# Query and key heads of one attention layer, normalized and rotated with tokens on the partitions

## What is computed

```python
def rms_norm(x, g):
    y = xf * lax.rsqrt(jnp.mean(xf * xf, axis=-1, keepdims=True) + EPS)
    return (y * g.astype(jnp.float32)).astype(x.dtype)

def apply_axial_rope(x, cos, sin):
    xs = x.reshape(x.shape[:3] + (2, 2, HEAD_DIM // 4))
    x1, x2 = xs[..., 0, :], xs[..., 1, :]
    out = jnp.stack([x1 * c - x2 * s, x2 * c + x1 * s], axis=-2)

bg_l, cg_l, vc_l, q_l, k_l, v_l, gt_l = jnp.split(hx @ w_in[layer], SPLITS, axis=-1)
q_l, k_l, v_l = split_heads(q_l, k_l, v_l, q_norm_g[layer], k_norm_g[layer])
q_c, k_c, v_c = split_heads(q_c, k_c, v_c, q_norm_g[layer], k_norm_g[layer])
q_l = apply_axial_rope(q_l, cos, sin)
k_l = apply_axial_rope(k_l, cos, sin)
k_all = jnp.concatenate([k_c, k_l], axis=1)
o_l = latent_attention(q_l, k_all, v_all)
```

## Time and profile before

| | us |
|---|---|
| median of 3 runs | 1324.51 |
| lowest, highest | 1324.28, 1335.15 |
| the profiled execution's own time | 1324.45 |
| its span, first to last instruction | 1322.6 |
| PE busy | 1304.7 (99%) |
| DVE busy | 903.0 (68%) |
| ACT busy | 644.3 (49%) |
| POOL busy | 27.3 (2%) |

### The profile page before, as it was taken

One profiled execution on the slowest core, in us unless ns is written; L12 is line 12 of the kernel. 1 busy time (PEld: TensorE's weight loads), 2 busy tenths in 40 slices (PEclk: granted clock), 3 DMA queues, 4 the chain that ended last, 5 costly groups with the idle time before them and its releaser, 6 DMA issues. The chain is left out here.

```text
span 1322.6 us, 23508 instructions
## 1 busy us (share of the span) xinstructions
PE 1304.7 (99%) x9348; PEld 1210.0 (91%) x9348; DVE 903.0 (68%) x1455; ACT 644.3 (49%) x1027; POOL 27.3 (2%) x27
## 2 busy tenths in 40 slices
PE   9999999999999999999999999999999999999998
PEld 6788888888889999999999999989999999999998
DVE  4768775555658587554775555788887665689873
ACT  4622311222236345554555445666665765556552
POOL 0000000000010000000000000200000000100000
PEclk9999999999999999999999999999999999999999
DMA  9755555646635354545556665556546455436760
GB/s 358 270 186 191 191 191 192 222 159 215 204 107 161 111 159 130 159 128 160 178 155 194 190 201 174 171 159 184 148 143 181 128 174 176 145 112 208 217 197 33
DMA packets 201485, 230.20 MB, mean 174 GB/s; under 512 B 7073, under 2 KB 191649, under 8 KB 201377
## 3 DMA queue, kind: packets, MB, share of 16 engines
q1 hardware_dynamic: 201088, 228.42, 54.7%
q10 hardware_dynamic: 288, 0.28, 0.1%
HBM read 227.63 MB, written 1.05 MB: 173 GB/s over the span
## 5 line engine op out<-in xcount | busy, mean ns | idle before, releaser
L1105 PE MATMUL P<-XHB,WH 128*128 128x256 f32 (+1 forms) x1808 | 553.1, 306 | 7.4 <-DVE XLB L1784 3.9
L1106 PE MATMUL P<-XLB,WH 128*128 128x256 f32 (+1 forms) x1808 | 543.2, 300 | 0.0
L1107 PE MATMUL P<-XHB,WL 128*128 128x256 f32 (+1 forms) x1808 | 543.2, 300 | 0.0
L1988 DVE TENSOR_TENSOR WL<-W,WH 128x1024 fp32r<-128x1024 f32 x358 | 431.7, 1224 | 87.2 <-ACT WH L1565 87.0
L1565 ACT ACTIVATE WH<-W 128x1024 fp32r<-128x1024 f32 x358 | 369.0, 1042 | 249.3 <-PE P L1107 157.8
L1105 PEld LDWEIGHTS P<-XHB,WH 128*128 128x128 f32 x1808 | 340.0, 188 | 27.7 <-issue 8.2
L1106 PEld LDWEIGHTS P<-XLB,WH 128*128 128x128 f32 x1808 | 340.1, 188 | 15.2 <-issue 0.5
L1107 PEld LDWEIGHTS P<-XHB,WL 128*128 128x128 f32 x1808 | 340.2, 188 | 14.6
L1105 PE MATMUL P<-GH,WH 128*128 128x256 f32 (+1 forms) x372 | 121.2, 326 | 0.0
L1106 PE MATMUL P<-GL,WH 128*128 128x256 f32 (+1 forms) x372 | 120.6, 324 | 0.0
L1107 PE MATMUL P<-GH,WL 128*128 128x256 f32 (+1 forms) x372 | 120.6, 324 | 0.0
(11 more groups left out here) (322 smaller groups left out, 1797.3 us busy)
## 6 DMA issues: line engine op xcount, KB each, us to landing
W<-in_ffn_w_in SPq DMA_DIRECT2D x88, 512.0 KB, 4.8
W<-in_w_in_ab SPq DMA_DIRECT2D x72, 512.0 KB, 4.6
W<-in_w_modt SPq DMA_DIRECT2D x56, 512.0 KB, 3.9
W<-in_w_in SPq DMA_DIRECT2D x52, 512.0 KB, 4.1
W<-in_ffn_w_out SPq DMA_DIRECT2D x40, 512.0 KB, 4.8
W<-in_w_in_c SPq DMA_DIRECT2D x32, 512.0 KB, 4.3
W<-in_w_out_ab SPq DMA_DIRECT2D x16, 512.0 KB, 4.4
W<-in_w_out_c SPq DMA_DIRECT2D x16, 512.0 KB, 4.7
```

Of the source, the lines that this page charges most:

```text
L1105: pe.matmul(o, h[:, k, c], xh[:, kk, a:b], start=kk == 0, stop=False)
L1106: pe.matmul(o, h[:, k, c], xl[:, kk, a:b], start=False, stop=False)
L1107: mm = pe.matmul(o, l[:, k, c], xh[:, kk, a:b], start=False, stop=kk == gm.nk - 1)
L1988: dve.tensor_tensor(l, a, h.bitcast(F32), ALU.subtract).then_inc(S["wl"], 1)
```

## The change

q and k are now made with the tokens on the partitions (`turned=False`: the activation is the stationary operand, the weights stream), as v was already. The columns of the weights are permuted on the host so that the swap of the rotation is a reversal of two halves of 64 along the row. The norm of a head is now a sum along the row. `qk_norm(u)` handles one gemm at a time (u = 0 to 3: two query heads, two token blocks; u = 4: both key heads, four token blocks) and is appended after q 0, q 1, q 2, q 3 and v:

- `qs`: ACT squares 128x128 pieces with an accumulated row sum (4 for a unit of q, 8 for k), then one root over 4 or 8 columns.
- `qr`: DVE takes a small reciprocal, then for each rotated piece a product with the sine table (halves reversed, into MC) and a product with the cosine table (in place); four of each. For k also four products with the gain alone. All are scalar_tensor_tensor with the reciprocal as the per-partition scalar.
- POOL adds the two parts of the rotation, two adds of 128x256 for a unit, ten in all.
- `qt`: PE transposes the pieces back (4 of 128x128 for a unit of q, 4 for each key head, 24 in all) and waits before it for the unit's last add on POOL. ACT copies the result to Q or K, 128x512 each.

The tables (gain times sine and cosine) are made once by DVE in a step `qg`, during the last products of the feed-forward, from a new transfer of 128 x 512 numbers on SP's queue. The k gemm writes four tiles of 256 columns instead of two of 512. The one-hot tile and POOL's two memsets are gone.

The core of the diff:

```diff
-            if i % 2:
-                self.call(lambda i=i: self.back.append(self.qk_norm(i // 2)))
+            self.call(lambda i=i: self.back.append(self.qk_norm(i)))
         self.call(self.reach, "ctx")
-        self.gemm("k", 0, WIN, 0, 8, 4096, ALL, first=True)
+        self.gemm("k", 0, WIN, 0, 8, 4096, ALL, turned=False, first=True)
...
-    def qk_norm(self, s):
-        self.step("qs", a=s)
-        for _ in range(2):
+    def qk_norm(self, u):
+        self.step("qs", a=u)
+        yield
+        self.step("qr", a=u)
+        yield
+        yield
+        for v in range(2 if u == 4 else 1):
+            b, f = self.bank(self.up("qn"))
+            self.step("qt", a=u, b=v, bank=b, free=f)
+            for name in (("k", v),) if u == 4 else (("q", 2 * u), ("q", 2 * u + 1)):
+                self.ready.add(name)
+                self.end[name] = self.at("qn")
             yield
-        b, f = self.bank(self.up("qr"))
-        self.step("qa", a=s, bank=b, free=f)
-        for _ in range(3):
-            yield
-        todo = None
-        for i in range(4):
-            if todo is not None:
-                self.rope(*todo)
-                todo = None
-            b, f = self.bank(self.up("qn"))
-            self.step("qb", a=s, b=i, c=self.at("qn"), bank=b, free=f)
-            if s < 2 or i % 2:
-                todo = (s, i, self.at("qn"))
-            else:
-                self.ready.add(self.name(s, i))
-                self.end[self.name(s, i)] = self.at("qn")
-            yield
-            yield
-        if todo is not None:
-            self.rope(*todo)
-
...
+            sp.dma_start(GR, w["qkg"].partition_broadcast(128).rearrange("p o c -> p (o c)")).then_inc(SX[0], 16)
...
-                elif s.kind == "qa":
-                    pe.wait_ge(S["fill"], 2)
-                    for i in range(4):
-                        n = 4 * s.a + i
-                        pe.wait_ge(S["qs"], n + 1)
-                        pe.matmul(ps[:, 0:T], HOT[:, 3 - i:131 - i], SQ[:, n % 3, T * (n // 3 % 2):T * (n // 3 % 2) + T], start=i == 0,
-                                  stop=i == 3).then_inc(S["qh"], 1)
-                elif s.kind == "qb":
+                elif s.kind == "qt":
                     pe.wait_ge(SI[5], 16)
-                    if s.b == 0:
-                        pe.wait_ge(S["qi"], s.a + 1)
-                    pe.matmul(ps[:, 0:T], con("sel", 128 * s.b, 128 * s.b + 128),
-                              rows_of(s.a), start=True, stop=True).then_inc(S["qb"], 1)
-                elif s.kind == "rope":
-                    ap = head(s.a, s.b)[0]
-                    pe.wait_ge(S["qn"], s.c)
-                    pe.matmul(ps[:, 0:T], con("perm"), ap, start=True, stop=True).then_inc(S["rm"], 1)
+                    n = 4 if s.a == 4 else 2
+                    pe.wait_ge(S["rd"], 2 * s.a + 2)
+                    for h in (s.b,) if n == 4 else (0, 1):
+                        for j in range(n):
+                            c = 128 * j if n == 4 else 256 * h + 128 * j
+                            mm = pe.transpose(ps[:, c:c + 128], place(s.a, j)[:, 128 * h:128 * h + 128], con("id"))
+                    mm.then_inc(S["rm"], 1)
...
+                if name == "s2":
+                    for u in range(5):
+                        k = 4 if u == 4 else 2
+                        for j in (k - 2, k - 1):
+                            y, p = raws(u)[j][1], place(u, j)
+                            pool.wait_ge(S["ro"], 8 * u + 2 * k + 2 * (j % 2) + 2)
+                            pool.tensor_tensor(p, p, y, ALU.add).then_inc(S["rd"], 1)
...
@@ -1640,17 +1617,26 @@
                         square("s6", k, (X[:, k, 256:512], 1.0))
                 elif s.kind == "qs":
                     act.wait_ge(S["on"], stat["s2"][2] + 6)
-                    for i in range(4):
-                        ap, _, _, (name, v) = head(s.a, i)
-                        n = 4 * s.a + i
-                        act.wait_ge(S[name], v)
-                        if n >= 6:
-                            act.wait_ge(S["qh"], n - 5)
-                        act.activation(SQ[:, n % 3, T * (n // 3 % 2):T * (n // 3 % 2) + T], ap, ACT.Square).then_inc(S["qs"], 1)
-                elif s.kind == "qa":
-                    act.wait_ge(S["qh"], 4 * s.a + 4)
-                    act.activation(rows_of(s.a), ps[:, 0:T], ACT.Sqrt, scale=1.0 / 128, bias=con("eps")) \
+                    n = 4 * s.a
+                    for j, y in raws(s.a):
+                        act.wait_ge(S["ke" if s.a == 4 else "qe"], j + 1 if s.a == 4 else 2 * s.a + j + 1)
+                        for h in range(2):
+                            if n >= 12:
+                                act.wait_ge(S["qs"], n - 11)
+                            act.activation(SQ[:, n // 4 % 3, 128 * (n % 4):128 * (n % 4) + 128], y[:, 128 * h:128 * h + 128],
+                                           ACT.Square, accum_out=RQ[:, n:n + 1]).then_inc(S["qs"], 1)
+                            n += 1
+                    act.wait_ge(S["qs"], n)
+                    act.activation(RQ[:, 4 * s.a:n], RQ[:, 4 * s.a:n], ACT.Sqrt, scale=1.0 / 128, bias=con("eps")) \
                         .then_inc(S["qr"], 1)
+                elif s.kind == "qt":
+                    if s.a < 4:
+                        act.wait_ge(S["rm"], s.a + 1)
+                        act.activation(Q[:, 2 * s.a:2 * s.a + 2, :], ps.rearrange("p (h t) -> p h t", h=2), ACT.Copy) \
+                            .then_inc(S["qn"], 1)
+                    else:
+                        act.wait_ge(S["rm"], 6)
+                        act.activation(K[:, s.b, :], ps, ACT.Copy).then_inc(S["qn"], 1)
...
-                elif s.kind == "qa":
-                    r = rows_of(s.a)
-                    dve.wait_ge(S["qr"], s.a + 1)
-                    dve.reciprocal(r, r).then_inc(S["qi"], 1)
-                elif s.kind == "qb":
-                    ap, gain, _, _ = head(s.a, s.b)
-                    dve.wait_ge(S["qb"], s.c)
-                    dve.scalar_tensor_tensor(ap, ap, gain, ps[:, 0:T], ALU.mult, ALU.mult).then_inc(S["qn"], 1)
-                elif s.kind == "rope":
-                    n, ap = s.k0, head(s.a, s.b)[0]
-                    tmp = TS[:, 3, T * (n % 2):T * (n % 2) + T]
-                    dve.wait_ge(S["rm"], n)
-                    dve.tensor_tensor(tmp, ps[:, 0:T], con("sin"), ALU.mult).then_inc(S["ro"], 1)
-                    dve.wait_ge(S["qn"], s.c)
-                    dve.tensor_tensor(ap, ap, con("cos"), ALU.mult).then_inc(S["dv"], 1)
+                elif s.kind == "qg":
+                    dve.wait_ge(SI[5], 16)
+                    dve.wait_ge(SX[0], 48)
+                    dve.wait_ge(S["md"], 56)
+                    for n in range(4):
+                        tg = dve.tensor_tensor(GT[:, n, :].rearrange("p (j d) -> p j d", j=2),
+                                               con(("cos", "sin")[n % 2]).rearrange("p (j d) -> p j d", j=2),
+                                               GR[:, 128 * n:128 * n + 128].unsqueeze(1).to_broadcast([128, 2, 128]), ALU.mult)
+                    tg.then_inc(S["qi"], 1)
+                elif s.kind == "qr":
+                    u = s.a
+                    n, k = (8, 4) if u == 4 else (4, 2)
+                    rq = RQ[:, 4 * u:4 * u + n]
+                    dve.wait_ge(S["qr"], u + 1)
+                    dve.reciprocal(rq, rq).then_inc(S["dv"], 1)
                     own += 1
                     dve.wait_ge(S["dv"], own)
-                    dve.wait_ge(S["ro"], n)
-                    dve.tensor_tensor(ap, ap, tmp, ALU.add).then_inc(S["rd"], 1)
+                    dve.wait_ge(S["qi"], 1)
+                    if u >= 2:
+                        dve.wait_ge(S["rm"], 4 if u == 4 else u - 1)
+                    heads, g = [(j, h) for j in range(k) for h in range(2)], 2 * (u // 4)
+                    for j, h in heads:
+                        d, t = slice(128 * h, 128 * h + 128), 128 * (j % 2)
+                        r, y, p = rq[:, 2 * j + h:2 * j + h + 1], raws(u)[j][1][:, d], place(u, j)[:, d]
+                        if j < k - 2:
+                            dve.scalar_tensor_tensor(p, y, r, GR[:, 256:384], ALU.mult, ALU.mult).then_inc(S["ro"], 1)
+                        else:
+                            p, y, sn = (v.rearrange("p (e c) -> p e c", e=2) for v in (p, y, GT[:, g + 1, t:t + 128]))
+                            dve.scalar_tensor_tensor(p, y[:, ::-1, :], r, sn, ALU.mult, ALU.mult).then_inc(S["ro"], 1)
+                    for j, h in heads[-4:]:
+                        d, t = slice(128 * h, 128 * h + 128), 128 * (j % 2)
+                        y = raws(u)[j][1][:, d]
+                        if h == 0:
+                            dve.wait_ge(S["ro"], 8 * u + 2 * k - 4 + 2 * (j % 2) + 2)
+                        dve.scalar_tensor_tensor(y, y, rq[:, 2 * j + h:2 * j + h + 1], GT[:, g, t:t + 128], ALU.mult,
```

(1 more changed line is left out.)

70 lines of the change are left out of this document (30 added, 40 removed).

## The result

| | before | changed |
|---|---|---|
| median of 9 runs, us | 1324.51 | 1339.25 |
| lowest | 1324.21 | 1338.63 |
| ratio, 95% interval | | 1.0111 (1.009 to 1.0131) |

The changed kernel is slower, 14.7 us in the medians. The predicted 1329 had the sign, but a third of the size (+5), and the time lies 1.45 us above the range's end of 1337.8. The profiled execution of the changed kernel took 1347.03 us, 7.8 above the median.

What follows compares the result with a forecast made beforehand. PE was taken as the bound, busy for 240.00 of 240.00 us from 400 to 640 us. 1324.5 - 11.9 (PE's work) + 14.8 (waits) + 2 (clock) = 1329.4, rounded 1329; range 1320 to 1338.

Steps and rivals of the forecast that it cites:

- PE's own work: On PE, 34 float32 matmuls go (14.6 us) and 24 transposes come (2.7 us): 11.9 us less.
- waits at the transposes: PE waits for POOL's last add before units 0 to 4: 2.3, 7.2 (units 1 and 2), 1.5 and 3.8, together 14.8 us.
- clock behind them: PE's clock falls once, after the wait of 6 us, costing 2 us (0 to 2.8); a second fall only possible.
- forecast A: The forecast itself: the new waits take back what PE saves, 1322 to 1336 us, chance 0.67.
- 275 ns: The Trainium skill's price of one 128x128 transpose on PE; by it 24 cost 6.6 us and PE's work falls 8.0.
- What remains on POOL behind DVE's last product: End of each unit's chain before its transposes: POOL's adds and a signal, 1.6 us, bounds 1.1 and 2.2.
- Rival D: DVE and POOL hinder each other: waits grow 6 us, a second clock fall adds 2.8, 1338 us; chance 0.10.
- B: Chains before the transposes are shorter than counted: waits 7.4 us, clock stays up, 1320 (or 1312 to 1321.5); chance 0.18.
- C: Everything is hidden at the transposes, as the rotation was before: 1312.6 us, chance 0.05.
- The attention's earlier start: First score about 20 us earlier; prediction called wrong if this opens or fills idle time on PE.
- the k gemm costs nothing: k turns from 48 matmuls of 512 columns at 0.24 us into 96 of 256 at 0.12: no cost.

Runs made afterwards that it cites:

- e10_after_again: The changed kernel, unchanged, profiled a second time: 1340.63 us.
- e1_fill: The changed kernel plus float32 filler products of constants on PE ahead of its waits for POOL: fastest 1337.08 us, ratio 1.0106 to before.
- e5_dveadd: The changed kernel with its ten additions on DVE instead of POOL, same order of steps: fastest 1327.87 us, ratio 1.0047 to before.
- e4_pause: The kernel before with one artificial wait of PE ahead of k, for 14 additions on POOL: fastest 1340.05 us, ratio 1.0126 to before.
- e2_late: The changed kernel with all transposes later in the planner's list, DVE steps of later units held back: fastest 1322.32 us, ratio 1.0007 to before.
- e6_late2: As e2_late, but units 1 to 3 start behind the context norm, their transposes within k and v: fastest 1318.51 us, ratio 0.998 to before.
- e9_late3: e6_late2 with k's first chunk going block by block instead of row by row: median 1319.69 us, fastest 1318.43, ratio 0.9956 to before.
- e7_late2d: e6_late2 with the additions on DVE instead of POOL: fastest 1318.94 us, median 1322.76, ratio 0.9968.

## Why the prediction was wrong

Step by step, with e10_after_again's trace against that of before:

| step | predicted | measured |
|---|---|---|
| PE's own work | -11.9 | -11.6 |
| waits at the transposes | +14.8 | +16.9 |
| clock behind them | +2 | +6.3 |
| spacing in the attention | 0 | +3.1 |
| sum | +4.9 | +14.7 |
| the stage in the traces | | +15.2 |
| medians | | +14.7 |

(0.5 us of the stage is in no term, so that the sum meets the medians is in part luck. That profile's span is 15.8 above before's: 0.5 of it is lost in the first 20 us, 0.1 behind the stage.) The sum of the prediction, 1329.4, is 9.9 short: 4.3 for the clock, 3.1 for the spacing, 2.1 for the waits and 0.3 for the work.

- **PE's own work** was right, and so was the mechanism, forecast A: the new waits take the saving back. Four transposes at the full clock take 0.44, as in the earlier trace rows. The 275 ns that the prediction set against this do not disagree with the trace: the profile shows 273 ns as the mean duration of a transpose at line 1237. But transposes overlap, so that the duration is not what one costs.
- **The waits** by unit were forecast at 2.3, 1, 6, 1.5 and 3.8, and measured at 2.7, 1.3, 6.9, 0 and 5.8 (with the time to start again behind each, 16.9 in all). What remains on POOL behind DVE's last product was put at 1.6 (at most 2.2). To the end of the second addition it was 1.7 for units 0, 1 and 3, 2.2 for unit 2 and 3.5 for unit 4, which is why unit 4 was 2 us short. An addition was taken at 1.0 and took 3.30 there, beside two splits without a gap between them; the upper bound, 1.26, was the mean of two beside one split and two shorter operations. For unit 3 no wait came, because slow products of k stood before it. e1_fill shows 3.3 us there once they are fast. So errors partly cancel in the sum of the waits: unit 3 did not wait, and the others waited longer than forecast.
- **The clock** is the step that failed: the term of 2 us measured 6.3. One fall was counted, behind the 6 us. The clock also fell behind waits of 2.7 and 5.8 us, and not behind 1.3. The prediction had named the last one as possible and left it out of the sum. The price of one fall (2, at most 2.8) was right: 1.5, 2.3 and 2.5 us by the distances at half rate. Part of it would have been waiting anyway (e1_fill).
- **Rival D** (DVE and POOL hinder each other) had a chance of 0.10 and was priced as the reason for a time of 1338 and more. Its mechanism is real: e5_dveadd takes 5.7 us of waits away by moving ten additions to DVE, and e4_pause shows DVE's norm products at twice their time. The forecast and this rival were no alternatives, both acted. But its price was not met: beyond the forecast it put 6 us on the waits, where 2.1 came, 2.8 on the clock, where 4.3 came, and nothing on the spacing, which took 3.1. That its 1338 is near the measured time is luck.
- **Spacing** of the products was in neither a term nor a bound. The 0.118 and the 0.113 both stand in the trace of before (the earlier trace rows has 0.12).
- **The attention's earlier start** (480.0 us in place of 492.4) opened no idle time, as said. That the k gemm costs nothing holds for its columns only. Its four banks cost 3.4 to 4.5 us where the transposes' wait does not stand in front (e2_late, e6_late2, with q 3's eviction late on ACT), and 1.1 with its tiles in another order (e9_late3).
- Rivals **B** and **C** fell. C's 1312.6 was not reached with an order made for the layout either: e9_late3 has PE without a wait over 1.1 us in this stage and keeps 7.3 of the 11.9 us.

## What to carry to other kernels

When work moves from the busiest engine to others, it is the position of the hand-back in that engine's order that decides: here the same operations make 1339 or 1320, by where 24 transposes and the steps ahead of them stand and by the order of k's tiles. Count a fall of the clock behind every wait of a few microseconds and not only behind the longest (here behind 2.7 us, and once not behind 3.3), and look at how many PSUM banks a gemm takes at its start when its tiles change form. A step given to an idle POOL is not free if both engines then read SBUF at the same time; price its operations by rows where DVE is busy throughout, one by one and not by the mean of a pair.

## What the chip showed beside that

- Products of 256 columns run at a distance of 0.113 or 0.118 us for a whole stage, at a granted clock of 1.00 and with PE busy throughout. For the second feed-forward it differs between executions of one kernel (884 and 851 products in the same 100 us), for the attention both kernels that were profiled twice repeated theirs. It is worth 3 to 7 us a stage and it hides differences of that size in a median.
- A norm product of DVE with two inputs in SBUF took twice its time (0.92 instead of 0.44 us) with additions on POOL back to back, a reciprocal with one input did not (1.74 and 1.75). An addition on POOL took 0.78 us where a product of DVE was held up (0.83 instead of 0.34), and 1.64 and 3.30 beside one and two splits.
- The granted clock fell behind waits of 2.7, 2.9, 3.4 and 3.7 us (the last two at k in e6_late2 and e7_late2d) and behind all longer ones. It did not fall behind 1.1, 1.2 and 1.3 us, nor behind the 3.3 of e1_fill.
- Fillers on PE (6.2 us of them in place of a wait of 6.9 us) did hold the clock at 1.00, and gave back only a part of what the lower clock had seemed to cost.
